# A hybrid decoder layer: finer expert widths, 16-bit dispatch tables, division ahead of the turning, idle products

## The reference

```
h    = rmsnorm(x);  proj = h @ w_in                 # u, gate, q, k, v, forget logits
rec  = rg_lru(u, gate)                              # conv, two gates, recurrence, 512 channels
att  = softmax(q k / 8 + c_q - c_k, causal) @ v     # 8 heads of 64, q and k normed, c = cumsum(log f)
x    = x + [rmsnorm(rec), rmsnorm(att)] @ w_out
h    = rmsnorm(x);  logits = h @ w_router + b       # 32 experts
top 4 of 32, gates = softmax(top values)
y_e  = ((clip(u)+1) * g*sigmoid(1.702 g)) @ w_down[e] + b_down[e],  [g, u] = h @ w_gate_up[e] + b
x    = x + sum over the token's 4 experts of gate * y_e
```

## Time and profile before

| | |
|---|---|
| median of 3 runs (lowest to highest) | 2010.98 us (2010.34 to 2013.39) |
| profiled execution, its time | 2016.19 us |
| its span, first to last instruction | 2014.4 us |
| TensorE busy | 1896.6 us, 94% |
| VectorE, ACT, POOL busy | 1276.9, 1050.2, 399.2 us |
| bytes moved | 478.76 MB, 238 GB/s over the span |
| mean granted TensorE clock | 0.977 of full speed |

### The profile page before, as it was taken

How to read it: one execution, slowest core, us unless ns; L and a number is a source line. 1 busy time by engine, 2 the same in 40 slices (tenths; PEclk the granted TensorE clock), 3 DMA queues, 4 the chain that set the end, 5 groups by cost and what they waited for, 6 DMA issues and landing times.

```text
span 2014.4 us, 51108 instructions
## 1 busy us (share of the span) xinstructions
PE 1896.6 (94%) x20629; PEld 1755.8 (87%) x20629; DVE 1276.9 (63%) x2642; ACT 1050.2 (52%) x1442; POOL 399.2 (20%) x302
## 2 busy tenths in 40 slices
PE   6999988989967999999999999999999999999895
PEld 4777756658857999999999999999999999999895
DVE  4553636765377555556666666567767767767865
ACT  5575425543114445455555555566656656656554
POOL 4000000001002111112111122222333333333423
PEclk9999989999978999999999999999999999999998
DMA  4111010005457777788888889998999999999992
GB/s 143 43 52 42 21 63 1 2 1 181 157 197 260 239 268 271 270 274 286 294 297 294 295 286 326 323 324 287 356 349 364 351 359 368 352 356 365 355 364 71
DMA packets 251385, 478.76 MB, mean 238 GB/s; under 512 B 17312, under 2 KB 38096, under 8 KB 251264
## 3 DMA queue, kind: packets, MB, share of 16 engines
q1 hardware_dynamic: 231040, 443.59, 61.1%
q0 software_dynamic: 20256, 33.94, 7.6%
HBM read 466.96 MB, written 47.19 MB: 255 GB/s over the span
## 4 chain that ended last, share of the span: by engine, by line
PE 55%; DVE 7%; issue 5%; ACT 2%; DVEq 0%; POOL 0%; ACTq 0%; POOLq 0%
PE E_p_d L1943 23%; PE E_p_g L1932 5%; PE E_p_g L1935 5%; PE E_p_g L1934 5%; PE E_p_u L1932 5%; PE E_p_u L1935 5%; PE E_p_u L1934 5%; DVE E_w_lo L1773 4%; PE E_p_t L1914 2%; PE E_p_t L1899 2%; ACT E_w_hi L1687 1%; DVE E_up L1833 1%; DVE E_gate L1821 1%; DVE E_gate L1827 1%; DVE E_peak L1767 0%
## 5 line engine op out<-in xcount | busy, mean ns | idle before, releaser
L1773 DVE SCALAR_TENSOR_TENSOR E_w_lo<-E_w_st,E_w_hi 128x2048 f16<-128x2048 f32 x260 | 594.7, 2287 | 60.3 <-ACT E_w_hi L1687 56.6
L1687 ACT ACTIVATE E_w_hi<-E_w_st 128x2048 f16<-128x2048 f32 x260 | 492.6, 1905 | 143.6 <-PE E_p_g L1935 96.7
L1943 PE MATMUL E_p_d<-E_a_f,E_w_st 128*128 128x160 f32 (+6 forms) x4096 | 531.0, 288 | 16.8 <-DVE E_a_f L1843 16.8
L1943 PEld LDWEIGHTS E_p_d<-E_a_f,E_w_st 128*128 128x128 f32 x4096 | 515.2, 191 | 25.0 <-issue 14.9
L1932 PE MATMUL E_p_g<-E_x_hi,E_w_hi 128*128 128x160 f16 (+6 forms) x2048 | 372.9, 224 | 8.3 <-issue 8.3
L1932 PE MATMUL E_p_u<-E_x_hi,E_w_hi 128*128 128x160 f16 (+6 forms) x2048 | 371.7, 223 | 5.0 <-DVE E_w_lo L1773 5.0
L1934 PE MATMUL E_p_g<-E_x_lo,E_w_hi 128*128 128x160 f16 (+6 forms) x2048 | 372.9, 224 | 0.0
L1935 PE MATMUL E_p_g<-E_x_hi,E_w_lo 128*128 128x160 f16 (+6 forms) x2048 | 372.9, 224 | 0.0
L1935 PE MATMUL E_p_u<-E_x_hi,E_w_lo 128*128 128x160 f16 (+6 forms) x2048 | 371.6, 223 | 0.0
L1934 PE MATMUL E_p_u<-E_x_lo,E_w_hi 128*128 128x160 f16 (+6 forms) x2048 | 371.6, 223 | 0.0
L1631 POOL DMA_INDIRECT out<-E_y_rows,E_idx_out x66 | 168.4, 2552 | 590.6 <-ACT E_y_rows L1705 566.0
(11 more groups left out here) (375 smaller groups left out, 2761.0 us busy)
## 6 DMA issues: line engine op xcount, KB each, us to landing
E_w_st<-in_w_gate_up SPq DMA_DIRECT2D x130, 2048.0 KB, 10.0
E_w_st<-in_w_down SPq DMA_DIRECT2D x64, 2048.0 KB, 14.6
A_w_st<-in_w_in SPq DMA_DIRECT2D x20, 512.0 KB, 3.9
A_x_rows<-in_x SPq DMA_DIRECT2D x8, 512.0 KB, 8.8
C_x_res<-in_x SPq DMA_DIRECT2D x8, 512.0 KB, 4.5
x_rows<-C_x SPq DMA_DIRECT2D x8, 512.0 KB, 5.0
out<-C_x SPq DMA_DIRECT2D x8, 512.0 KB, 5.8
h_rows<-C_h SPq DMA_DIRECT2D x8, 512.0 KB, 4.5
```

What stands on the lines that cost most here:

```text
L1687: act.activation(w_hi[c % RI][:], staged(c % NG), ACT.Copy, scale=SW).then_inc(hi_s, 1)
L1773: dve.scalar_tensor_tensor(out=w_lo[c % RI][:], in0=staged(c % NG), scalar=SW, in1=w_hi[c % RI][:], op0=ALU.mult, op1=ALU.subtract, accum_ ...
L1943: ins = pe.matmul(banks[:, h, 0:w], staged(c)[:, k, h * P:(h + 1) * P], x[:, k, 0:w], start=h == 0 and k == 0, stop=k == KT - 1, skip_grou ...
```

## The change

- **E**: four more widths (184, 168, 152, 136); `GROUP` and `FINE` are constants for what follows. Each class has its own code. Twelve idle products of 512 columns stand ahead of the first item on TensorE.
- **D**: the tables and all that they are made of are 16-bit, laid out in groups of 8 choices with the 8 innermost; the gates go as a high and a low 16-bit part, scaled by 2 to the 15th. 28 idle products stand ahead of the table products.
- **B**: each tile is divided by its row sum before it is turned, on VectorE (tile n) or ACT (tiles n+1 to n+3). The spread of the inverses and the multiplication behind it are gone. The slim tiles are turned into the second `p_o` bank. The order on each engine changes. The mean square is one column per block, inverted once at the end.
- **C**: the root is of 8 columns; TensorE spreads it over `p_m` by products with the identity, from where VectorE reads it. Eight idle products stand around the last turning. The count of chosen experts is reduced straight to bfloat16.

```diff
-WIDTHS = (256, 192, 176, 160, 144, 128, 112, 96)
+WIDTHS = (256, 192, 184, 176, 168, 160, 152, 144, 136, 128, 112, 96)
+GROUP = 8
+FINE = 8
...
 stage_b, TensorE
+        def home_of(n):
+            return p_o[1] if n % 4 >= 2 else p_t
...
             def turn(n):
-                pe.wait_ge(exp_s, n + 1)
...
+                if n % 4:
+                    pe.wait_ge(norm_act, 3 * (n // 4) + n % 4)
+                else:
+                    pe.wait_ge(norm_dve, n // 4 + 1)
...
             def weigh(u, side):
-                pe.wait_ge(inv_s, u + 1)
...
-                for e in range(2):
-                    pe.matmul(p_o[0][e * HD:(e + 1) * HD, o + P:o + 2 * P],
-                              row_inv[:, n + e:n + e + 1].to_broadcast([P, HD]), m.ident[:], start=True, stop=True)
...
             for u in range(NU):
...
                 turn(n)
                 if u:
                     weigh(u - 1, 1)
+                turn(n + 2)
                 turn(n + 1)
                 if u + 1 < NU:
                     score_pair(n + 6)
-                turn(n + 2)
-                weigh(u, 0)
                 turn(n + 3)
                 if u % 4 == 1 and u > 4:
                     sums(u // 4 - 1)
+                weigh(u, 0)
...
 stage_b, ACT
+            def normal(n):
+                L = P * (where(n)[0] + 1)
+                act.wait_ge(inv_s, 2 * (n // 4) + 1 + n % 4 // 2)
+                act.activation(tile_of(n)[:, 0:L], tile_of(n)[:, 0:L], ACT.Copy, scale=row_inv[:, n:n + 1]
+                               ).then_inc(norm_act, 1)
...
             for u in range(NU):
                 n = 4 * u
+                normal(n + 2)
+                normal(n + 3)
                 keep_turned(n)
+                keep_turned(n + 2)
                 if u + 1 < NU:
                     exps(n + 4)
                     exps(n + 5)
-                keep_turned(n + 2)
-                if u + 1 < NU:
                     exps(n + 6)
                     exps(n + 7)
+                    normal(n + 5)
...
 stage_b, VectorE
+            def normal(n):
+                L = P * (where(n)[0] + 1)
+                dve.wait_ge(inv_s, 2 * (n // 4) + 1)
+                dve.tensor_scalar(tile_of(n)[:, 0:L], tile_of(n)[:, 0:L], row_inv[:, n:n + 1], None,
+                                  ALU.mult).then_inc(norm_dve, 1)
...
 stage_c, ACT and TensorE
-            act.activation(att_rs[:], m.att_ms[:], ACT.Sqrt).then_inc(att_ok, 1)
+                if g == 1:
+                    act.activation(att_rs[:], m.att_ms[:], ACT.Sqrt).then_inc(att_ok, 1)
...
             rec_part(0)
+            pe.wait_ge(att_ok, 1)
+            for t in range(T):
+                ins = pe.matmul(p_m[t // 4][:, t % 4 * P:(t % 4 + 1) * P], att_rs[:, t:t + 1].to_broadcast([P, P]), m.ident[:],
+                                start=True, stop=True)
+                if t % 4 == 3:
+                    ins.then_inc(rs_mm, 1)
...
             route(T - 2)
+            pe.wait_ge(x2_s, T - 1)
+            keep_warm(3)
             turn(T - 1)
+            keep_warm(5)
             route(T - 1)
...
 stage_d, VectorE and TensorE
+            for g in range(NG):
+                step(dve.tensor_tensor(one_hi[:, g], m.iota_hi[:], spread(hi_f[:], SLOTB), ALU.is_equal))
+                dve.tensor_tensor(one_lo[:, g], m.iota_lo[:], spread(lo_f[:], P), ALU.is_equal)
+                dve.tensor_tensor(val_row[:, g], one_hi[:, g], spread(m.row_no[:], SLOTB), ALU.mult).then_inc(row_s, 1)
...
+            for g in range(NG):
+                dve.tensor_tensor(val_gate[:, g, 0], one_hi[:, g], spread(ex_hi[:], SLOTB), ALU.mult)
+                dve.tensor_tensor(val_gate[:, g, 1], one_hi[:, g], spread(ex_lo[:], SLOTB), ALU.mult).then_inc(gate_s, 1)
...
+            for _ in range(28):
+                pe.matmul(p_warm[:], m.ident_b[:], m.ident_b[:].unsqueeze(1).to_broadcast([P, 4, P]), start=True, stop=True)
             for q in range(TK):
-                pe.wait_ge(row_s, q + 1)
-                ins = pe.matmul(p_row[:], one_lo[:, q, :], val_row[:, q, :], start=q == 0, stop=q == TK - 1)
+                g, n = q // GROUP, q % GROUP
+                pe.wait_ge(row_s, g + 1)
+                ins = pe.matmul(p_row[:], one_lo[:, g, :, n], val_row[:, g, :, n], start=q == 0, stop=q == TK - 1)
...
 stage_e, TensorE
+                if fast:
+
+                    for _ in range(12):
+                        pe.matmul(p_u[1][:].rearrange("p a n -> p (a n)"), m.ident_b[:],
+                                  m.ident_b[:].unsqueeze(1).to_broadcast([P, 4, P]), start=True, stop=True)
```

More of the change, by code:

```diff
@@ L783, in score_pair @@
                     pe.wait_ge(score_s, n)
+                u = n // 4
+                if n % 4 == 0 and u % 4 == 3 and u > 4:
+                    pe.wait_ge(ms_s, (u - 2) // 4)
                 for c0 in range(0, L, 512):
@@ L833, in sums @@
                     pe.wait_ge(ms_s, q)
-                for c in range(CT):
-                    ins = pe.matmul(p_o[1][:, 0:2 * P], m.rec_ones[:], square[:, c, :], start=c == 0, stop=c == CT - 1)
+                for side in range(2):
+                    for c in range(CT):
+                        ins = pe.matmul(p_s[0][:, 512 + side:513 + side], square[:, c, side * P:(side + 1) * P],
+                                        m.rec_ones[:, 0:1], start=c == 0, stop=c == CT - 1, skip_group_check=True)
                 ins.then_inc(sum_mm, 1)
@@ L969, in mean @@
                 for side in range(2):
-                    ins = dve.tensor_scalar(m.att_ms[:, rows_of(q, side)], p_o[1][:, side * P:(side + 1) * P], EPS, None,
-                                            ALU.add)
+                    i = blocks[q][side]
+                    ins = dve.tensor_scalar(m.att_ms[:, i:i + 1], p_s[0][:, 512 + side:513 + side], EPS, None, ALU.add)
                 ins.then_inc(ms_s, 1)
-                dve.wait_ge(ms_s, q + 1)
-                for side in range(2):
-                    step(dve.reciprocal(m.att_ms[:, rows_of(q, side)], m.att_ms[:, rows_of(q, side)]))
             key_rows(0)
@@ L983, in _ @@
             key_rows(6)
+            inverse(0)
+            normal(0)
             for u in range(NU):
                 n = 4 * u
-                inverse(u)
+                inverse(n + 2)
                 if u + 1 < NU:
@@ L995, in _ @@
                     subtract(n + 7)
+                    inverse(n + 4)
+                    normal(n + 4)
+                keep_turned(n + 3)
+                if u % 4 == 1 and u > 4:
+                    mean(u // 4 - 1)
                 out_rows(u, 0)
-                keep_turned(n + 3)
                 if u % 2 and u // 2 < KT - 2:
@@ L1002, in _ @@
                                       ALU.subtract).then_inc(wo_lo_s, 1)
-                if u % 4 == 1 and u > 4:
-                    mean(u // 4 - 1)
             out_rows(NU - 1, 1)
             mean(T // 2 - 1)
+            dve.wait_ge(ms_s, T // 2)
+            step(dve.reciprocal(m.att_ms[:], m.att_ms[:]))
 def stage_c(nc, m, a):
@@ L1091, in _ @@
             step(pool.memset(m.limit[:, 0:1], float(CHUNK)))
+            for v in range(1, NV):
+                if WIDTHS[v] != WIDTHS[1] - FINE * (v - 1):
+                    step(pool.memset(m.limit[:, v:v + 1], float(WIDTHS[v])))
             pool.memset(m.ones_f[:], 1.0).then_inc(tables, 1)
@@ L1251, in stage_d @@
     TK = T * TOPK
-    GROUP = 8
+    NG = TK // GROUP
+    UP = 2.0 ** 15
     with ExitStack() as ctx:
@@ L1257, in at @@
         def at(name, shape, dt):
-            n = 4
+            n = 2 if dt == F16 else 4
             for s_ in shape[1:]:
@@ L1404, in _ @@
             dve.tensor_copy(m.rows_in[:], ids_f[:]).then_inc(rows_in_s, 1)
-            ex_q = ex[:].rearrange("p t k -> p (t k)")
-            for q in range(TK):
-                dve.tensor_scalar(val_gate[:, q, :], m.iota_hi[:], hi_f[:, q:q + 1], ex_q[:, q:q + 1],
-                                  ALU.is_equal, ALU.mult).then_inc(gate_s, 1)
+            step(dve.tensor_copy(ex_hi[:], ex_q))
+            step(dve.tensor_tensor(ex_lo[:], ex_q, ex_hi[:], ALU.subtract))
+            for g in range(NG):
+                dve.tensor_tensor(val_gate[:, g, 0], one_hi[:, g], spread(ex_hi[:], SLOTB), ALU.mult)
+                dve.tensor_tensor(val_gate[:, g, 1], one_hi[:, g], spread(ex_lo[:], SLOTB), ALU.mult).then_inc(gate_s, 1)
             step(dve.tensor_tensor(sums_f[:], ids_f[:], m.spare[:].rearrange("p a b -> p (a b)"), ALU.min))
@@ L1412, in _ @@
             dve.wait_ge(gate_mm, 1)
-            step(dve.tensor_copy(m.gates[:], p_gate[:]))
+            step(dve.tensor_scalar(low_part[:], p_gate[:, 1, :], 1.0 / UP, None, ALU.mult))
+            step(dve.scalar_tensor_tensor(out=m.gates[:], in0=p_gate[:, 0, :], scalar=1.0 / UP, in1=low_part[:],
+                                          op0=ALU.mult, op1=ALU.add))
         @block.tensor
```

121 lines of the change are left out of this document (67 added, 54 removed).

## The result

The changed kernel takes 1991.8 us (median of four runs, 1990.7 to 1993.1) against 2010.7 us of the kernel before (2010.2 to 2013.4, same set): a ratio of 0.9904, interval [0.9886, 0.9921], 19 us faster. A second set gave 0.9877 [0.9862, 0.9892], 24 us. The forecast was 1976 us, with a range of 1961 to 1991. Profile against profile, 2016.2 us became 1991.9, so 24.3 us; the sum had 35.2.

The account below looks back on a forecast made before the run. TensorE's expert products, timed by their width, bound 1400 of 2014 us, behind three serial stages. -16.3 (E), 0 (start), -5.5 (D), -15.5 (B), +4.1 - 2 (C) make -35.2: 2016.2 to 1981.0, less 5.2: 1976 us, range 1961 to 1991.

Parts of the forecast that it names:

- D: Stage ahead of the experts: 16-bit tables on VectorE bring the experts' first turning 5.5 us sooner, ends -6.5 and +1.3.
- B: Attention: division ahead of the turning takes 16 units from 9.13 to 8.35 us, -12.5, and the tail -3.
- C: Stage between attention and tables: start +4.1 us for root and spreads, tail -2 by idle products and a dropped cast.
- the sum: All stage terms added: -35.2 us, from the profiled 2016.2 to 1981.0 us.
- E's start: Up to the first expert product: second jump +1.5, faster clock -1.5, in sum 0, ends -2.4 and +9 us.
- the last subtraction: 5.2 us taken off 1981.0 to get from the profiled run to the median of the runs, giving 1976.
- E's widths: Expert items: twelve widths in place of eight shrink eight items by 8 columns, -16.3 us, ends -12.5 and -17.
- the second jump: Experts' start: TensorE jumps past empty classes 256 and 192, not 256 alone; taken as +1.5 us, ends 0 and +4.2.
- The doubt about the clock: Experts' start: 3 us idle still lie between idle products and first product, so -1.5 us, of 2.4 at most.
- rival on the late start: Start of the experts: the jump waits for the idle products and costs twice, +9 us, time 1985; chance 0.12.
- rival on class entries: Experts: nine class entries each pay 4.2 or 8.3 us, 38 or 75 us, time 2014 or 2051; chance 0.03.
- TensorE reads every eighth element slowly: Half of the rival that the 16-bit tables are no faster: table stage 1.3 us longer, time 1983; chance 0.15.

Follow-up runs that it names:

- one jump: The changed kernel without the width 192, which no item has, so one empty class lies ahead of the first item: ratio 0.9823.
- jump and order: The changed kernel without width 192 and with the rest of the output weights (wo_lo) issued behind the next unit's inverse on VectorE: 1977.2 us, ratio 0.9807.
- d_more_idle: The changed kernel with 36 idle products ahead of the row products and 12 more between row and gate products: ratio 0.9886.

## Why the forecast missed

The forecast missed by some 16 us (1991.8 for 1976): 4.0 in B, 4.0 in D, 2.5 at E's start, 1.5 in E's items and 5.2 by the last subtraction, less 1.0 that A and C gave more than forecast.

**E's widths: right.** 49.75, 45.50 and 42.64 for 49.7, 45.6 and 41.7 us; -14.6 to -14.8 in place of -16.3, inside the ends given. The 136-wide items make up the difference: both take 42.6, 1.0 less than at 144 and not 1.9, because TensorE waits once for VectorE.

**E's start: the jump mis-sized, the clock wrong.** The sum had "I take +1.5" for the second jump, and -1.5 for the clock. The jump costs 5.8 to 6.0 us at this place and the clock another 2.1, because the longer wait lets it fall: +2.5 by the table, for 0 forecast, but against the same kernel with one jump 8.1. The end of +4.2 for the jump was read from the kernel before, where one jump left 4.2 us uncovered; a jump's price isn't the same in another layout of the code. Taken whole, at 4.2 us, the jump would have given +2.7 for the +2.5 of the table, with the clock's -1.5 still wrong. The doubt about the clock, 3 us of idle time behind the idle products, was the right one; the gap was 7 us. Of the rival on the late start one half came true, a second jump at the full price (4.2 said, 5.8 measured); the jump doesn't wait for the idle products. The rival on class entries priced nine of them, where by its own count three are new; the runs put an entry behind a used class at nothing, so it doesn't matter here.

**D: the mechanism right on one engine, wrong on the next.** VectorE's tables came at the very times forecast. The sum treated TensorE as free ("products that VectorE paces anyway") and left the strided read to a rival, "TensorE reads every eighth element slowly", priced at +1.3. Half of this rival came true: the row index came 5.1 us sooner, but the gates held the end, -1.5 net for -5.5. The layout was in the diff and could be counted: 32 products of 196 columns at a step of 16 bytes, for which the trace had no price; they took 11.5 us. With the step mended, the first turning came 5.7 us earlier than before counted from D's start (35.1 for 40.8): the forecast 5.5.

**B: the mechanism right, one wait missed.** 8.65 us a unit for 8.35, by the copies -7.2 us over fifteen units where -12.5 was put down for sixteen; what follows the last copy gave 4.7 (14.6 to 9.9) for 3. The forecast looked at what the divisions push back, and not at what they newly wait for: an inverse behind wo_lo, which waits for ACT itself. Without that ring the stage is 15.3 us shorter than before, for 15.5.

**C: right in the sum, each part a little smaller.** +3.3 for +4.1 at the start and -0.8 to -1.9 for -2 in the tail.

**The last subtraction was wrong.** 5.2 us were taken off because one profiled run lay that far above its median. That was the clock's form in one execution; the changed kernel's profile was in that same form and so, it seems, are most of its runs, so nothing was to be taken off, and 1981 would have been the sum. Which form the changed kernel would take nobody could read from the trace of before. With jump and order mended the kernel's profile ends at 1977.9 us, 36.5 under that of before. That this is so near to 35.2 is in part luck: E's start (-3.2, for 0) makes up for D (-1.8, for -5.5). But the change holds such a gain, and two of its own details gave a third of it back.

## What to carry to other kernels

When data is laid out for one engine, write down the step that every other reader of it sees, in bytes: here 4 bytes suited both, 16 cost TensorE a factor of 2.2 at half clock and 4 at full, and a repeated innermost element cost VectorE 1.8. A class or branch that is empty at the head of a loop isn't free (3.5 to 5.8 us here, by what looks like the fetch of code), so a table of cases starts with a case that is used. Before moving work onto an engine, follow what the new instruction waits for back to that same engine, and don't carry the distance of one profiled run from its median into a forecast.

## What was not expected of the hardware

- 32 products with operands at a step of 16 bytes take 11.46 to 11.50 us at 0.50 of the clock and partly at 1.00 of it alike: this pace doesn't follow TensorE's clock.
- The clock fell at 590.2 us in `d_more_idle` with TensorE busy by the profile all the time from 580.2, on those slow products; and in the changed kernel, 1.3 us of idle time behind the 28 idle products, it fell at 579.9 although the row products ran.
- Two executions of one program differ by 5 us through the place where the clock falls in the first 30 us and behind the border of two stages.
